# Attention in units of two maps, norms on two engines instead of three, and the first two weight tiles of a sub-layer side by side

## What is computed

```python
h = modulate(rms_norm(x, norm_g[l, 0]), sh1, sc1)       # "pre" norm
x = x + gt1 * rms_norm(mixer(h), norm_g[l, 1])          # "post" norm
h = modulate(rms_norm(x, norm_g[l, 2]), sh2, sc2)
x = x + gt2 * rms_norm(swiglu(h, w_gate_up, w_down), norm_g[l, 3])
```

```python
s = einsum('bqhmd,bthmd->bhmqt', dq, dk) * 64 ** -0.5
p = softmax(s);  a = p[:, :, 0] - lam * p[:, :, 1];  d_out = rms_norm(a @ dv, subln_g) * (1 - lam_init)
p = softmax(einsum('bqgrd,btgd->bgrqt', gq, gk) * 64 ** -0.5);  g_out = p @ gv
y = concat(d_out, g_out) @ w_out
```

## Time and profile before

| | value |
|---|---|
| median of three runs | 1403.09 us |
| the profiled execution | 1406.29 us |
| its span, first to last instruction | 1404.2 us |
| PE busy | 1243.1 us (89%) |
| DVE, ACT, POOL busy | 664.8, 573.0, 183.4 us |
| mean granted TensorE clock | 0.939 of full speed |

### The profile page before, as it was taken

One profiled execution on the slowest core, in us unless ns is written; L12 is line 12 of the kernel. 1 busy time (PEld: TensorE's weight loads), 2 busy tenths in 40 slices (PEclk: granted clock), 3 DMA queues, 4 the chain that ended last, 5 costly groups with the idle time before them and its releaser, 6 DMA issues.

```text
span 1404.2 us, 19657 instructions
## 1 busy us (share of the span) xinstructions
PE 1243.1 (89%) x7965; PEld 1013.4 (72%) x7965; DVE 664.8 (47%) x1016; ACT 573.0 (41%) x1003; POOL 183.4 (13%) x170
## 2 busy tenths in 40 slices
PE   5699989998949999999999579968758977999996
PEld 3377755566828888888888258867657966999996
DVE  2433257554373232333222564559955556555444
ACT  2322246444343222323222346555374635444542
POOL 0120320100041111111000310010011432111101
PEclk9899999999969999999999779988967999999998
DMA  7555555775303333333333112223101214466661
...
DMA packets 239140, 159.63 MB, mean 114 GB/s; under 512 B 14522, under 2 KB 213580, under 8 KB 239052
## 3 DMA queue, kind: packets, MB, share of 16 engines
...
...
## 4 chain that ended last, share of the span: by engine, by line
PE 76%; DVE 13%; ACT 5%; issue 2%; DMA 2%; POOL 1%; ACTq 0%; SPq 0%; DVEq 0%; POOLq 0%
PE bank L1331 55%; PE bank L1319 3%; PE bank L1456 2%; PE bank L1479 2%; PE bank L1370 2%; DVE w_lo L1736 2%; DVE h_lo L1783 1%; DVE xT L1806 1%; PE bank L1464 1%; PE bank L1301 1%; DVE blocks L995 1%; PE bank L754 1%; DVE outer L993 1%; DVE conv_out L1071 1%; DVE h_hi L1782 1%
## 5 line engine op out<-in xcount | busy, mean ns | idle before, releaser
L1331 PE MATMUL bank<-h_hi,w_hi 128*128 128x512 f32 (+2 forms) x1240 | 442.9, 357 | 63.5 <-DVE h_lo L1783 33.9
L1331 PE MATMUL bank<-h_lo,w_hi 128*128 128x512 f32 (+2 forms) x1240 | 434.7, 351 | 0.0
L1331 PE MATMUL bank<-h_hi,w_lo 128*128 128x512 f32 (+2 forms) x1240 | 434.2, 350 | 0.0
L1736 DVE TENSOR_TENSOR w_lo<-w_raw,w_hi 128x1024 fp32r<-128x1024 f32 (+1 forms) x203 | 249.8, 1232 | 307.1 <-ACT w_hi L1540 306.4
L1331 PEld LDWEIGHTS bank<-h_hi,w_hi 128*128 128x128 f32 (+1 forms) x1240 | 242.2, 195 | 105.5 <-issue 63.9
L1331 PEld LDWEIGHTS bank<-h_hi,w_lo 128*128 128x128 f32 (+1 forms) x1240 | 242.6, 196 | 29.7 <-issue 1.0
L1331 PEld LDWEIGHTS bank<-h_lo,w_hi 128*128 128x128 f32 (+1 forms) x1240 | 243.1, 196 | 27.0 <-issue 0.5
L1540 ACT ACTIVATE w_hi<-w_raw 128x1024 fp32r<-128x1024 f32 (+1 forms) x203 | 209.7, 1037 | 102.0 <-PE bank L1331 84.6
L1331 PE MATMUL bank<-act_hi,w_hi 128*128 128x512 f32 (+1 forms) x352 | 118.3, 336 | 0.0
L1331 PE MATMUL bank<-act_lo,w_hi 128*128 128x512 f32 (+1 forms) x352 | 118.3, 336 | 0.0
L1331 PE MATMUL bank<-act_hi,w_lo 128*128 128x512 f32 (+1 forms) x352 | 118.3, 336 | 0.0
...
## 6 DMA issues: line engine op xcount, KB each, us to landing
...
```

Source lines behind the costliest of these rows:

```text
L1331: m = nc.tensor.matmul(dst, stationary(a, k), moving(b, k), start=(first and k == kk[0] and a == b == 0), stop=(last and k == kk[-1] and a ...
L1736: nc.vector.tensor_tensor(w_lo[where[key] % N_RAW][:, 0:tiles, 0:w], raw_slot(key)[:, 0:tiles, 0:w], w_hi[m % N_SPLIT][:, 0:tiles, 0:w].bi ...
```

## The change

**Attention.** The units become 32, (tile of two maps, block of 128 queries). A differential tile is a head as before, a plain tile is two heads, one of either key/value head. Queries and keys of the two maps lie on partitions 0 to 63 and 64 to 127, and each score product reads only its own 64 partitions; the zeroed query copies go, and POOL writes the query tile once. Plain units turn two maps, and their values are products of 64 output rows each, written to the two halves of one bank. Attention takes its banks from a ring of six ("att"), and the values from a single bank 7 ("out"). Ada chunks go in pairs in three of every four steps (48 chunks), and the last 14 go into the first FFN, in pairs behind every second of its first 14 gate/up products. The output weights load in three DMAs a chunk, since the plain heads' rows are in another order, and their first split moves from step 44 of 52 to step 32 of 36.

**Norms.** POOL does nothing in them. The gate is applied by ACT when it copies `y` out of PSUM (per stream), DVE does `y * post_rstd` and the addition to `xT`, then all eight `xT * pre_rstd`, three tiles ahead of its `h_lo`; the rounding to `h_hi` moves from DVE to ACT.

**First products.** `project_two` makes the first two output tiles of a sub-layer together, six passes per feature tile.

```diff
-ATT_UNITS = [(head, qb) for head in range(DIFF_HEADS + GQA_HEADS) for qb in range(T // P)]
+ATT_UNITS = [(tile, qb) for tile in range(KT) for qb in range(T // P)]
...
-def maps_of(head):
-
-    if head < DIFF_HEADS:
-        return [(head, 0, 1 + head), (head, 1, 1 + head)]
-    g, r = divmod(head - DIFF_HEADS, GQA_HEADS // GQA_KV)
-    return [(DIFF_HEADS + r, g, 0)]
...
+def key_tile(tile):
+    return 1 + tile if tile < DIFF_HEADS else 0
+
+
+def turned_maps(tile):
+    return range(1 if tile < DIFF_HEADS else 2)
...
-    if phase == "att" and step % 3 and ATT_PAIR[step] < 31:
-        return pair(34, ATT_PAIR[step])
+    if phase == "att" and step % 4:
+        return pair(34, step - step // 4 - 1)
+    if phase == "gate0" and step % 2 and step < 14:
+        return pair(82, step // 2)
...
-            out += [("gate", layer, n)]
+            out += [("gate", layer, n)] + [("ada", a) for a in ada_after(f"gate{layer}", n)]
...
-        RINGS = {"work": (2, 3, 4, 5, 6), "side": (7, 1), "extra": (0, 7, 1), "core": (2, 3, 4, 5, 6, 7, 1, 0)}
-        taken = {"work": 0, "side": 0, "extra": 0, "core": 0}
+        RINGS = {"work": (2, 3, 4, 5, 6), "side": (7, 1), "att": (2, 3, 4, 5, 6, 1), "out": (7,), "extra": (0, 7, 1), "core": (2, 3, 4, 5, 6, 7, 1, 0)}
...
+            def project_two(first_of, lo, keys, widths=(P, P)):
+
+                dsts = [take(key)[0:width, lo:T] for key, width in zip(keys, widths)]
+                ws = [weights(key) for key in keys]
+                for k in range(KT):
+                    pe.wait_ge(h_ready, first_of * KT + k + 1)
+                    for key, dst, w, width in zip(keys, dsts, ws, widths):
+                        for a, b in ((0, 0), (0, 1), (1, 0)):
+                            m = nc.tensor.matmul(dst, w(a, k)[:, 0:width], (h_hi, h_lo)[b][:, k, lo:T],
+                                                 start=(k == a == b == 0), stop=(k == KT - 1 and a == 1))
+                        if k == KT - 1:
+                            finish(m, key)
...
-                for n in range(2 * FT):
-                    project(("gate", layer, n), ("gate", layer, n), lo, i if n == 0 else None)
+                project_two(i, lo, [("gate", layer, n) for n in range(2)])
+                for n in range(1, 2 * FT):
+                    if n > 1:
+                        project(("gate", layer, n), ("gate", layer, n), lo)
+                    ada(ada_after(f"gate{layer}", n))
...
-                head, qb = ATT_UNITS[n]
-                for m, (qt, half, kt) in enumerate(maps_of(head)):
-                    if qb == 0:
-                        pe.wait_ge(qk_out, 5 + qt + 1)
-                    dst = take(("s", n, m))
-                    finish(nc.tensor.matmul(dst[:, 0:keys_of(qb)], q_sb[:, qt, half, qb * P:(qb + 1) * P],
-                                            k_sb[:, kt, 0:keys_of(qb)], start=True, stop=True), ("s", n, m))
+                tile, qb = ATT_UNITS[n]
+                if qb == 0:
+                    pe.wait_ge(qk_out, 5 + tile + 1)
+                dsts = [take(("s", n, m), "att") for m in range(2)]
+                for m in range(2):
+                    half = slice(m * HEAD, (m + 1) * HEAD)
+                    finish(nc.tensor.matmul(dsts[m][:, 0:keys_of(qb)], q_sb[half, tile, qb * P:(qb + 1) * P],
+                                            k_sb[half, key_tile(tile), 0:keys_of(qb)], start=True, stop=True),
+                           ("s", n, m))
 
             def turn(n):
-                qb = ATT_UNITS[n][1]
+                tile, qb = ATT_UNITS[n]
                 pe.wait_ge(probs_ready, n + 1)
-                dst = take(("t", n))
-                for t in range(keys_of(qb) // P):
-                    m = nc.tensor.transpose(dst[:, t * P:(t + 1) * P],
-                                            probs[:, n % 3, 0, t * P:(t + 1) * P], ident)
-                finish(m, ("t", n))
+                for m in turned_maps(tile):
+                    dst = take(("t", n, m), "att")
+                    for t in range(keys_of(qb) // P):
+                        last = nc.tensor.transpose(dst[:, t * P:(t + 1) * P],
+                                                   probs[:, n % 3, m, t * P:(t + 1) * P], ident)
+                    finish(last, ("t", n, m))
...
-                    take(("o", head), "side")
-                dst = bank(("o", head))
-                wait_evacuated(pe, ("t", n))
-                c0 = head * P if head < DIFF_HEADS else 512 + (head - DIFF_HEADS) // 4 * P
+                    take(("o", tile), "out")
+                dst = bank(("o", tile))
+                for m in turned_maps(tile):
+                    wait_evacuated(pe, ("t", n, m))
                 tiles = keys_of(qb) // P
                 for t in range(tiles):
-                    m = nc.tensor.matmul(dst[:, qb * P:(qb + 1) * P], v_sb[:, t, c0:c0 + P],
-                                         probsT[:, n % 2, t, :], start=(t == 0), stop=(t == tiles - 1))
-                finish(m, ("v", n))
-                done_at[("o", head)] = jobs[0]
+                    if tile < DIFF_HEADS:
+                        last = nc.tensor.matmul(dst[:, qb * P:(qb + 1) * P], v_sb[:, t, tile * P:(tile + 1) * P],
+                                                probsT[:, n % 2, 0, t, :], start=(t == 0), stop=(t == tiles - 1))
+                        continue
+                    for m in range(2):
+                        c0 = DIFF_HEADS * P + m * HEAD
+                        last = nc.tensor.matmul(dst[m * HEAD:(m + 1) * HEAD, qb * P:(qb + 1) * P],
+                                                v_sb[:, t, c0:c0 + HEAD], probsT[:, n % 2, m, t, :],
+                                                start=(t == 0), stop=(t == tiles - 1))
...
+                for k in range(KT + 1):
+                    if k < KT:
+                        act.wait_ge(pre_scaled, i * KT + k + 1)
+                        for s in range(lo // CTX, 2):
+                            a, b = STREAMS[s]
+                            last = nc.scalar.activation(h_work[:, k, a:b], h_work[:, k, a:b],
+                                                        ACT.Identity, scale=mod_col(layer, part + 1, k, s),
+                                                        bias=mod_col(layer, part, k, s))
+                        last.then_inc(h32_ready, 1)
+                    if k:
+                        act.wait_ge(h32_ready, i * KT + k)
+                        nc.scalar.activation(h_hi[:, k - 1, lo:T], h_work[:, k - 1, lo:T],
+                                             ACT.Copy).then_inc(h_hi_ready, 1)
...
+                if m == 0:
+                    act.wait_ge(mods_ready, i // 2 * 4 + (4 if i % 2 else 2))
                 nc.scalar.activation(post_views[i][1][:, m % 2, lo:T], bank(("y", i, m))[:, lo:T], ACT.Square)
-                release(nc.scalar.activation(y_views[i][:, m, lo:T], bank(("y", i, m))[:, lo:T], ACT.Copy),
-                        ("y", i, m))
+                for s in range(lo // CTX, 2):
+                    a, b = STREAMS[s]
+                    last = nc.scalar.activation(y_views[i][:, m, a:b], bank(("y", i, m))[:, a:b], ACT.Copy,
+                                                scale=mod_col(i // 2, 3 * (i % 2) + 2, m, s))
+                release(last, ("y", i, m))
...
-                for k in range(KT):
-                    if (k + 1) in SCALED_BY_VECTOR["pre"]:
-                        scale_pre(dve, i, k + 1, True)
-                    dve.wait_ge(h32_ready, i * KT + k + 1)
-                    link(nc.vector.tensor_copy(h_hi[:, k, lo:T], h_work[:, k, lo:T]))
-                    nc.vector.tensor_tensor(h_lo[:, k, lo:T], h_work[:, k, lo:T],
-                                            h_hi[:, k, lo:T].bitcast(F32), ALU.subtract).then_inc(h_ready, 1)
+                wait_evacuated(dve, ("pre", i))
+                for k in range(KT + AHEAD):
+                    if k < KT:
+                        nc.vector.tensor_tensor(h_work[:, k, lo:T], xT[:, k, lo:T], pre_rstd[:, lo:T],
+                                                ALU.mult).then_inc(pre_scaled, 1)
+                    if k >= AHEAD:
+                        m = k - AHEAD
+                        dve.wait_ge(h_hi_ready, i * KT + m + 1)
+                        nc.vector.tensor_tensor(h_lo[:, m, lo:T], h_work[:, m, lo:T],
+                                                h_hi[:, m, lo:T].bitcast(F32), ALU.subtract).then_inc(h_ready, 1)
...
-                layer, part = i // 2, 3 * (i % 2) + 2
-                dve.wait_ge(mods_ready, layer * 4 + (4 if i % 2 else 2))
-                for k in range(KT):
-                    if k + 1 in SCALED_BY_VECTOR["post"]:
-                        scale_post(dve, i, k + 1, True)
-                    wait_scaled(dve, "post", i, k)
-                    for s in range(first_out(i) // CTX, 2):
-                        a, b = STREAMS[s]
-                        last = nc.vector.scalar_tensor_tensor(
```

(23 more changed lines are left out.)

179 lines of the change are left out of this document (67 added, 112 removed).

## The result

The changed kernel took 1368.62 us (median of four runs, 1366.1 to 1374.86), beside 1404.64 us for the kernel before on the same chip (1401.18 to 1406.68). The ratio is 0.9753, 95% interval 0.971 to 0.9795: 2.5% faster. The forecast was 1364, range 1343 to 1389.

A forecast was written before the change was run, and what follows sets the result against it. PE was taken to bound attention and the first FFN, a chain over all engines the norms. Gains of 51.3 us less 12 lost gave 39.3, taking the median 1403.1 to 1364 us, range 1343 to 1389.

The forecast's parts named there:

- Side by side: Attention: two half-array products cost one if overlapped; scores 20.6 us (41.2 without overlap), 64-row values 10.8 (21.5 without).
- Three slots: Rival, attention scores: strict start order makes a product pair take three slots of 0.43 us, +10.3, 1374 us; chance 0.12.
- no overlap: Rival, attention: scores and 64-row values do not run side by side, +31 us, 1395 us; chance 0.07.
- Changes of shape: Attention: PE changes how it uses the array 68 times more, at 0.11 us each, 7.5 us.
- The stage of 124.7: Attention window after the change, 124.7 us: 96.0 work, 7.5 shape changes, 3 bank waits, 16.2 carried over, 2 for DVE.
- the old 16.2: Attention: 16.2 us of ramp, tail and waits in the old stage, carried over unchanged into the new sum.
- The rival of a unit's chain: Attention: waits in a unit set the step, differential 3.8 us, double plain 5.0; +16 us, 1380 us; chance 0.18.
- Bank of the head statistic: Attention: four sums of squares take a bank from the old ring, so PE waits; 3 us in all.
- DVE in the way: Attention: 2 us added because DVE keeps 90 of its 95.2 us in a shorter stage.
- Start of attention: Before DVE's first maxima: POOL writes one query copy per tile instead of two, gaining 2 us (0 to 3).
- Ada in the FFN: First FFN: seven pairs of ada chunks moved there lose 12 us, nothing hiding them; bounds 10 and 14.
- Norms: Norms and first products: gains of 8.3 us before the first FFN, 9.2 before GDN, 3.7 in the latent-only norms.

The follow-up runs named there:

- the run with the same rows: The changed kernel with both score products of a unit reading rows 0 to 63 of queries and keys (scores wrong); 1386.05 us, one run.
- experiment 7: The changed kernel with VectorE's part of the head norm one step later than ScalarE's part; 1359.71 us, ratio 0.9702 to the kernel before.
- experiment 6: The changed kernel with both score products of a unit reading all 128 rows of queries and keys (scores wrong); 1373.51 us, one run.

## Why the prediction was right

The time came within 5 us. Most terms held; one, the attention's waits, was wrong in a way that only the experiments show. That the sum still came out is partly luck: the span shrank by 39.5 us where 39.3 were forecast, because attention took 4.4 us more than its sum and the norms and GDN, of which GDN was not touched, some 6 less than theirs.

- *Side by side.* Right in mechanism and size: a pair of score products holds PE for 1.06 us (0.86 in two slots plus 0.2), 16 half-width value passes for 1.03. Three slots and no overlap are both out; the run with the same rows shows what no overlap looks like, +17.3 us of attention.
- *Changes of shape.* 68 at 0.11 were 7.5 us. The 0.2 in each of 32 score pairs is 6.4, and 0.12 more in each of 16 plain steps 1.8: 8.2. Right within 1 us.
- *The stage of 124.7.* The term that failed is "the old 16.2", the ramp, tail and waits of the old attention, carried over as if they could not change. They did: the head norm's wait, which cost the old units 4.4 us, costs the new ones 10, about half of it through the clock. Without it the stage took 119.1 (experiment 7), 5.6 below my sum, and with it 129.1, 4.4 above. The rival of a unit's chain had the kind of cause right (a wait behind which the maxima stand), with its 0.18, but at the wrong place: it gave plain steps 5.0 us, and they took 4.0, while differential ones took 4.1. I had put PE's waits down as covered because each has a whole step of PE behind it. In a differential step the change halves the score passes. That they were the cover is not shown: at this wait PE stood 0.8 us before and 2.0 after, but also 1.7 with the long passes of experiment 6. Named waits of PE in the attention came to 12.7 us, below the 20 that would have told against the forecast. And I named no price for the clock in the attention at all.
- *Bank of the head statistic.* 3 us taken; the trace shows PE waiting there once, 0.8 us; what the other ring is worth by itself was not separated from POOL's part.
- *DVE in the way.* 2 us for DVE's share; it worked 85.4 us, not 90, but its wait for scores stayed, 24.8 us in 15 waits against 31.8 in 30. "DVE no longer waiting long" was wrong. In the differential half (total us, times, longest) the longest wait, 4.5 us, ended at 230.45, after the score pair at half clock:

```profile
DVE stats L1882 <- PE bank L1438: 11.7, 7, 4.5
```

- *Start of attention.* 2 us foretold, 0.1 found. I counted POOL's instructions, not their form: one with a constant takes 1.49, as long as the two with operands that it replaces (1.5 for a pair). The 1.2 us in the table lie ahead of QKV's last pass (177.19 before, 176.14 after), so they are not from here; what gave them is not shown.
- *Ada in the FFN.* 12 against 12.5, nothing hid it.
- *Norms.* 8.3, 9.2 and 3.7 against 9.7, 11.6 and 3.7. What was mis-sized is the time at half clock: 5.5 us taken, 2.7 measured (passes of 0.63 from 384.26 to 386.9), with 48 passes in 12.5 us, 13.5 by my sum. Before GDN my own two ends, 826.0 and 816.6, give 9.4 and not 9.2; the other 2 us there are not accounted for.
